# A down projection by seven products: the first product of each chunk copied by ScalarE from one set of PSUM banks to the other instead of being added to X on its own

## What is computed

```python
x = x + concat([retention(...), mla(...)]) @ w_o
h = rmsnorm(x, ffn_norm_g)
x = x + (silu(h @ w_ffn_gate) * (h @ w_ffn_up)) @ w_ffn_down      # D_FF = 2816
gate = sigmoid(rmsnorm(x, ple_norm_g) @ w_ple_gate)
x = x + gate * (p @ w_ple_proj)
return rmsnorm(x, final_norm_g)
```

## Time and profile before

| | us |
|---|---|
| median of 3 runs | 1298.08 (1297.96 to 1299.14) |
| the profiled execution, its own time | 1301.71 |
| its span in the trace | 1299.9 |
| PE busy | 1252.5 (96% of the span) |
| VectorE busy | 732.6 (56%) |
| ScalarE busy | 489.5 (38%) |
| GpSimd busy | 486.9 (37%) |

### The profile page before, as it was taken

The page is one execution under the profiler, slowest core; times in us unless marked ns, Lnnn a source line. Parts: engine busy times, 40 slices in busy tenths (PEclk is TensorE's granted clock), DMA queues, the critical chain, the costliest instruction groups (busy, mean ns, idle before and its releaser), DMA issues.

```text
span 1299.9 us, 17340 instructions
## 1 busy us (share of the span) xinstructions
PE 1252.5 (96%) x6052; PEld 1053.0 (81%) x6052; DVE 732.6 (56%) x1203; ACT 489.5 (38%) x896; POOL 486.9 (37%) x502
## 2 busy tenths in 40 slices
PE   6999989988999999989999999999999999999997
PEld 6888878877888788878888888888888878788886
DVE  4634444456666415854454544445479999974434
ACT  5732222235665403533333333333344443424422
POOL 2323333432000002552455543345379887710001
PEclk9999999989999999999999999999999999999999
DMA  6411111010003400042332332233255545330002
GB/s 206 136 33 50 33 33 48 0 41 1 1 16 114 146 1 1 1 139 68 111 122 93 110 122 89 82 114 122 102 206 178 183 174 177 114 113 1 1 33 97
DMA packets 101685, 110.81 MB, mean 85 GB/s; under 512 B 4848, under 2 KB 68720, under 8 KB 101616
## 3 DMA queue, kind: packets, MB, share of 16 engines
q1 hardware_dynamic: 101328, 109.38, 26.1%
q10 hardware_dynamic: 288, 0.52, 0.1%
HBM read 86.29 MB, written 23.59 MB: 85 GB/s over the span
## 4 chain that ended last, share of the span: by engine, by line
PE 75%; issue 13%; POOL 5%; DVE 3%; ACT 1%; DMA 1%; POOLq 0%; SPq 0%; ACTq 0%; DVEq 0%
PE PS L1531 10%; PE PS L1533 10%; PE PS L1532 10%; PE PS L1865 4%; PE PS L1867 4%; PE PS L1866 4%; PE PS L204 3%; PE PS L880 3%; PE PS L206 3%; PE PS L205 3%; PE PS L896 3%; PE PS L2223 2%; PE PS L2224 2%; PE PS L2222 2%; PE PS L2233 2%
## 5 line engine op out<-in xcount | busy, mean ns | idle before, releaser
L204 PE MATMUL PS<-WF,HTH 128*128 128x512 f32 (+1 forms) x448 | 178.1, 398 | 2.5 <-ACT X L338 1.8
L206 PE MATMUL PS<-WF,HTL 128*128 128x512 f32 (+1 forms) x448 | 174.5, 390 | 0.0
L205 PE MATMUL PS<-WF,HTH 128*128 128x512 f32 (+1 forms) x448 | 174.3, 389 | 0.0
L1252 DVE TENSOR_TENSOR X<-X,PS 128x512 f32<-128x512 f32 x172 | 110.0, 678 | 67.6 <-PE PS L206 52.6
L1533 PE MATMUL PS<-HTH,WF 128*128 128x512 f32 x336 | 130.7, 389 | 0.0
L1532 PE MATMUL PS<-HTL,WF 128*128 128x512 f32 x336 | 130.7, 389 | 0.0
L1531 PE MATMUL PS<-HTH,WF 128*128 128x512 f32 x336 | 130.7, 389 | 0.0
L1464 DVE TENSOR_TENSOR WF<-RAW,WF 128x512 fp32r<-128x512 f32 x63 | 69.7, 1107 | 83.1 <-ACT WF L1454 83.1
L1531 PE MATMUL PS<-WF 128*128 128x512 f32 x252 | 98.7, 392 | 3.9 <-issue 3.9
L204 PEld LDWEIGHTS PS<-WF,HTH 128*128 128x128 f32 x448 | 85.2, 190 | 18.0 <-issue 2.2
L1532 PE MATMUL PS<-WF 128*128 128x512 f32 x252 | 98.7, 392 | 0.0
(11 more groups left out here) (254 smaller groups left out, 2831.0 us busy)
## 6 DMA issues: line engine op xcount, KB each, us to landing
hid<-TMP SPq DMA_DIRECT2D x74, 256.0 KB, 2.3
TMP<-hid SPq DMA_DIRECT2D x25, 512.0 KB, 4.9
RAW<-in_w_ffn_gate SPq DMA_DIRECT2D x22, 512.0 KB, 4.1
RAW<-in_w_ffn_up SPq DMA_DIRECT2D x22, 512.0 KB, 5.3
RAW<-in_w_ffn_down SPq DMA_DIRECT2D x22, 512.0 KB, 4.2
X<-in_x SPq DMA_DIRECT2D x16, 512.0 KB, 4.6
RAW<-in_w_in SPq DMA_DIRECT2D x32, 256.0 KB, 3.2
TAB<-hid SPq DMA_DIRECT2D x9, 512.0 KB, 4.7
```

Of the source, the lines that this page charges most:

```text
L204: nc.tensor.matmul(dst, HTH[:, k, tok], w_h, start=(k == 0), stop=False)
L205: nc.tensor.matmul(dst, HTH[:, k, tok], w_l, start=False, stop=False)
L206: last = nc.tensor.matmul(dst, HTL[:, k, tok], w_h, start=False, stop=(k == K - 1))
L1252: nc.vector.tensor_tensor(x, x, src, ALU.add).then_inc(done, 1)
```

## The change

Step q = 0 is not added to `X` any more. ScalarE copies each of its four banks from set 0 to set 1 (`twice`), and step q = 1 accumulates upon the copy, without a fresh start. Its addition then brings both products to `X` at once. The step q = 3 accumulates in set 0 as before. PE's q = 1 waits for the copies (`f_twice`) in place of additions. The copies wait for the products of q = 0 and for the additions of q = 4 of the chunk before; in the first chunk they take over PE's waits for the last hidden block. `twice(c)` stands in ScalarE's list right behind `ring_hi(7c + 4)`. `N_ADDED` = 120 replaces 140 in the counts of additions behind.

```diff
+        N_ADDED = 4 * 6 * CHUNKS
+        def added(s, p):
+            return 4 * (s - s // 7 - 1) + p + 1
1068.40:1075.00 6.60, 6.37 (x27) 1.00 0.51 176
1114.50:1121.00 6.50, 6.23 (x26) 1.00 0.68 235 pe_step
             for p in range(4):
-                if before >= 0:
-                    e.wait_ge(f_added, 4 * before + p + 1)
+                if q == 1:
+                    e.wait_ge(f_twice, 4 * (s // 7) + p + 1)
+                elif before >= 0 and before % 7:
+                    e.wait_ge(f_added, added(before, p))
                 elif q == 0 and p == 2:
                     e.wait_ge(f_h0, NB - 1)
                     e.wait_ge(f_silu1, NB - 1)
-                elif q == 1 and p == 0:
-                    e.wait_ge(f_silu0, NB)
-                    e.wait_ge(f_silu1, NB)
-                    e.wait_ge(f_h0, NB)
...
-                    nc.tensor.matmul(dst, h_h, w_h, start=(q < 3 and k == 0), stop=False, skip_group_check=True)
+                    nc.tensor.matmul(dst, h_h, w_h, start=(q in (0, 2) and k == 0), stop=False, skip_group_check=True)
...
+        def twice(e, c):
+            s = 7 * c
+            if c == 0:
+                e.wait_ge(f_silu0, NB)
+                e.wait_ge(f_silu1, NB)
+                e.wait_ge(f_h0, NB)
+            for p in range(4):
+                e.wait_ge(f_down, 4 * s + p + 1)
+                if c:
+                    e.wait_ge(f_added, added(s - 3, p))
+                nc.scalar.copy(bank(DOWN_BANK[1][p]), bank(DOWN_BANK[0][p])).then_inc(f_twice, 1)
1068.40:1075.00 6.60, 6.37 (x27) 1.00 0.51 176
1114.50:1121.00 6.50, 6.23 (x26) 1.00 0.68 235 add_step
+            if q == 0:
+                return
...
-                e.wait_ge(f_added, 4 * (s - 1) + p + 1)
-            elif s == 1:
-                e.wait_ge(f_added, p + 1)
+                e.wait_ge(f_added, added(s, p) - 4)
1068.40:1075.00 6.60, 6.37 (x27) 1.00 0.51 176
1114.50:1121.00 6.50, 6.23 (x26) 1.00 0.68 235 act_5
             for u in range(2, STEPS):
                 ring_hi(e, u)
+                if u % 7 == 4:
+                    twice(e, u // 7)
```

More of the change, by code:

```diff
@@ L1070, in build @@
         s_d = [sem(f"s_d{i}") for i in range(4)]
-        d_hi, d_lo, f_down, f_added = sem("d_hi"), sem("d_lo"), sem("f_down"), sem("f_added")
+        d_hi, d_lo, f_down, f_added, f_twice = sem("d_hi"), sem("d_lo"), sem("f_down"), sem("f_added"), sem("f_twice")
         NB = FF // P
@@ L1902, in pe_down @@
                     if n < 4:
-                        e.wait_ge(f_added, N_DOWN - 1 if n == 0 else N_DOWN)
+                        e.wait_ge(f_added, N_ADDED - 1 if n == 0 else N_ADDED)
                     else:
-                        e.wait_ge(f_added, N_DOWN + n - 3)
+                        e.wait_ge(f_added, N_ADDED + n - 3)
                     dst = bank(4 + n % 4)
@@ L1939, in add_down @@
             e.wait_ge(f_down, N_DOWN + n + 1)
-            e.wait_ge(f_added, N_DOWN)
+            e.wait_ge(f_added, N_ADDED)
             add_x(e, bank(4 + n % 4), n // 2, (n % 2) * HALF, HALF, f_added)
@@ L2050, in ple_squares @@
         def ple_squares(e, t):
-            e.wait_ge(f_added, N_DOWN + 2 * t + 2)
+            e.wait_ge(f_added, N_ADDED + 2 * t + 2)
             if t == 0:
@@ L2208, in pe_6 @@
                 if u < 2:
-                    e.wait_ge(f_added, N_DOWN + 2 * T - 2 + 2 * u)
+                    e.wait_ge(f_added, N_ADDED + 2 * T - 2 + 2 * u)
                 if u >= 2:
```

## The result

| | before | changed |
|---|---|---|
| median of 6 runs, us | 1297.95 (1296.75 to 1299.14) | 1304.91 (1303.29 to 1308.68) |
| ratio to before, 95% interval | | 1.0058 (1.0043 to 1.0074) |
| the profiled execution, us, and its span | 1301.71, 1299.9 | 1304.02, 1301.3 |
| down stage, first to last matmul of its 35 steps | 958.11 to 1152.97 | 952.86 to 1154.34 |
| of that, lost against 839 intervals of 0.2267 us | 4.66 | 11.28 |

The change costs 0.58% by the ratio; the medians differ by 7.0 us. The two traced executions differ by only 1.4 us in their spans, because the changed one reached the down stage 5.25 us sooner, through code that is the same in both. Stretches ahead of the stage vary like that from execution to execution: a second trace of the kernel before began the stage at 957.54.

What follows compares the result with a forecast made beforehand. PE's matmuls bound the down stage, with VectorE additions costing 4.6 us of 195. Median 1298.08 plus 6.05 (stall), 1.7 (clock) and -0.6 (stalls at steps 20 and 28) gave 1305.2 us, range 1301.2 to 1308.5.

Steps and rivals of the forecast that it cites:

- The stall in chunk 0: Before step 1, PE waits for copies queued behind the cast of step 4's rows: +6.05 us, bounds 5.7 to 7.05.
- The clock: At PE's restart in step 1, a stretch at the 1.2 GHz level costs +1.7 us, bounds 0 and 3.4.
- The stalls at steps 20 and 28: PE's waits for VectorE additions at steps 20 and 28 stay, slightly shorter: -0.6 us, bounds -4.6 and about +0.9.
- The rival that VectorE bounds the stalls: With 12.4 us less VectorE work, both stalls at steps 20 and 28 go: -4.6 us, 1301.2 us in all, chance 0.14.
- The queue behind the copies: ring_hi(7c + 5) slips in four chunks: forecast cost nothing; rival, chance 0.06, up to 1.9 us a chunk, 1312.8 us.
- The sum: Whole kernel: stall in chunk 0, clock and stalls at steps 20 and 28 together +7.15 us, giving 1305.2 us, 0.55% slower.
- What was cited: Skill pages: activity releases PE's throttled clock; VectorE and GpSimd share an exclusive port lock, which fewer additions don't free.

Runs made afterwards that it cites:

- the two other kernels with the stall: Changed kernel with chunk 0 alone changed, ratio to before 1.0052; changed kernel with the copies of chunk 0 moved behind ring_hi(5), ratio 1.0076.

## Why the prediction was right, by its own steps

- **The stall in chunk 0.** Forecast 6.05 us, measured 6.27. (The row's 6.11 us are counted from the modelled end of the last matmul, 0.16 us behind the time at which the next should have started.) The chain is the one that was read from before: store, load, cast, four copies, step 1. The cast that waits for the load began 10.04 us behind step 0, and 9.83 in before, which makes up the difference. That the load landed so nearly as in before was not certain: the earlier trace rows has a longest time of 7.1 us, which would have made the stall 9.4 us, and the bound of 7.05 was drawn from the median.
- **The clock.** Charged at 1.7 with bounds 0 and 3.4. Measured 1.5 here, 2.8 and 2.1 in the two other kernels with the stall. The price was near, and its bounds were needed. Its reason was weak, and luck has a part in it. The prediction called the 3.86 us up to 572.87 the one idle time of this kind and went by length. But the same trace has 1.82 us up to 61.56 with a slow stretch behind it, and other traces have idle times of up to 3.45 us with none (last section). Behind the three stalls of 5.85 us and more for the copies the clock did fall each time.
- **The stalls at steps 20 and 28.** Forecast -0.6, measured -1.2: -0.9 at steps 20 to 22 (-0.35 was expected) and -0.3 at steps 28 and 29 (as expected). They are still there and still ended by additions:

```profile
1064.22 0.69 DVE L1252 TENSOR_TENSOR X<-X,PS 128x512 f32<-128x512 f32 x1 [0.25 <-PE PS L1870]
1064.83 4.47 DVE L182 SCALAR_TENSOR_TENSOR WF<-GB,GK,WF 128x512 fp32r<-128x512 f32 x2
1069.23 1.27 DVE L1252 TENSOR_TENSOR X<-X,PS 128x512 f32<-128x512 f32 x2
```

  `piece_lo` is issued 6.25 us behind the start of step 18 (1058.58), where it was 6.81 (1062.84 - 1056.03): 0.56 sooner, as worked out. That it took 4.47 us and not 4.82 was not; this is the mis-sized term. At 1064.22 VectorE waits for PE, so it carried no lag into `piece_lo`. That is why 22 us less work on it bought so little. The forecast had put the 0.56 down to the additions saved at step 14. The kernel with chunk 0 alone changed still makes them and got 0.8 us back at step 20, so this cause isn't shown. Of the 0.3 us at step 28 it got almost nothing (2.2 us lost against 2.3), which goes with the changed chunks.
- **The rival that VectorE bounds the stalls** fell as it was put: both stalls remained. But what it says of the freed time holds under a condition that the prediction did not see, that other work is moved into it (5.2 us of stage loss with `piece_lo` moved).
- **The queue behind the copies.** The casts of `ring_hi(12)` slipped from 5.8 us behind the start of step 7 to 6.1, and the steps behind lost nothing. No gap stands in chunks 1 to 4 that was not there before. Chunks 1 to 4 alone show it by their time.
- **The sum.** 6.05 + 1.7 - 0.6 = 7.15 forecast. In the trace of the stage 6.27 + 1.53 - 1.19 = 6.61, by the medians 7.0. The misses of the terms are 0.2 to 0.6 us each and partly cancel.
- **What was cited.** What the prediction took from the Trainium skill, "TensorE: Matmul & The Clock Gate" ("What's actually happening") and "SBUF — State Buffer" ("SBUF: two separate sides"), changed no number of the sum. The first agreed in kind again: the clock was at its lower level at all three restarts behind a stall for the copies. By the second, fewer additions free no time of the lock; both stalls stayed (3.5 of 4.7 us), which agrees better than the full 4.6 us would. But the `ring_lo` instructions did get 12.2 us shorter in all, which the prediction had not foreseen.

## What to carry to other kernels

When work is moved to an engine with time to spare, read what stands ahead of it in that engine's list and the latest thing that any of it waits for, in the first round of the loop above all: there, a load that nobody needed before step 4 became a wait of step 1. Time freed on an engine is worth something only between the place where it last waited for another and the place where it is late; here that meant moving the late work (`piece_lo`) onto the freed steps. And an in-order engine's queue is repaired by moving lines: the same four copies, two places sooner, took back 0.6%.

## What the runs showed of the hardware that was not expected

The clock did not follow the length of PE's idle time. Idle times of 1.33 and 1.46 us were followed by the full clock. In the kernel before with `piece_lo` moved, 2.15 us were followed by a restart below the full clock (columns as in group 14):

```profile
1081.08:1085.50 4.42, 4.42 (x12) 0.61 0.90 285
```

In the kernel with chunk 0 alone changed, 3.45 us up to 571.66 were followed by none:

```profile
571.66 0.47 PE L1531 MATMUL PS<-WF 128*128 128x512 f32 x1 [3.45 <-issue]
...
571.66:575.00 3.34, 3.34 (x15) 1.00 0.21 79
```

The idle time at this place, near 570 us, stands in all ten traces. Behind 2.40, 3.86 and 3.92 us a slow stretch followed, behind 2.06, 2.43, 2.66, 2.88, 2.94, 3.13 and 3.45 none. Even one kernel differs from execution to execution: the two traces of the kernel before both have an idle time of 1.82 us, up to 61.56 and up to 61.40, and only the first was followed by a slow stretch.

```profile
61.56:65.00 3.44, 3.44 (x9) 0.54 0.22 67
...
61.40:65.00 3.60, 3.60 (x16) 1.00 0.21 61
```

And a longer stall did not mean a dearer restart. Behind 5.85 us of waiting the clock cost 2.8 us, behind 6.11 us 1.5, and behind 8.35 us 2.1. The slow stretch behind the shortest of them still held at 971.5 and beyond, 5 us after the restart:

```profile
966.73:969.00 2.27, 2.27 (x6) 0.50 1.02 382
969.00:971.50 2.50, 2.50 (x7) 0.50 0.33 126
971.50:972.30 0.80, 0.80 (x3) 0.50 0.02 8
```

What decides whether the clock falls behind a stall, and for how long, was not tried.
